# A mixture-of-experts stage regrouped from units of 64 rows on two column halves to units of 32 rows on four column quarters

## The reference

```python
logits = xt @ router_w + router_b            # 32 experts
top_v, top_i = lax.top_k(logits, 4)          # 4 experts a token: 2048 rows in all
gates = softmax(top_v)
# for every expert e and its rows xb:
gu = xb @ w_gate_up[e] + b_gate_up[e]        # 1024 -> 2048, gate and linear interleaved
act = x_glu * sigmoid(1.702 * x_glu) * (x_lin + 1)      # both clipped at 7
out = act @ w_down[e] + b_down[e]            # 1024 -> 1024
# out rows times their gates, summed back to the tokens
```

## Time and profile before

| | |
|---|---|
| median of 3 runs | 1922.38 us |
| span of the profiled execution | 1919.6 us, which leaves 2.8 us around it |
| PE (matmul) busy | 1788.8 us, 93% |
| PEld (weight load) busy | 1106.8 us, 58% |
| DVE busy | 1025.5 us, 53% |
| ACT busy | 795.8 us, 41% |
| POOL busy | 236.5 us, 12% |
| mean DMA rate over the span | 270 GB/s, 494.10 MB read |

### The profile page before, as it was taken

One profiled execution on the slowest core, in us unless ns is written; L12 is line 12 of the kernel. 1 busy time (PEld: TensorE's weight loads), 2 busy tenths in 40 slices (PEclk: granted clock), 3 DMA queues, 4 the chain that ended last, 5 costly groups with the idle time before them and its releaser, 6 DMA issues. The chain is left out here.

```text
span 1919.6 us, 41921 instructions
## 1 busy us (share of the span) xinstructions
PE 1788.8 (93%) x14459; PEld 1106.8 (58%) x14459; DVE 1025.5 (53%) x1632; ACT 795.8 (41%) x1163; POOL 236.5 (12%) x302
## 2 busy tenths in 40 slices
PE   6999888599999999999999899999999769998897
PEld 3999654455555555555554455555555336777763
DVE  5794435554554555544544345545454473874655
ACT  5335523244444444444443344444444433533411
POOL 0000000111111111111111011111111220350000
PEclk9999999699999999999999899999999879999999
DMA  8881771449878997997599998999999662221011
GB/s 328 271 263 45 197 236 43 180 158 406 356 284 318 423 379 284 363 427 324 206 406 427 426 427 338 421 427 372 405 427 426 260 211 68 77 77 46 21 40 44
DMA packets 129708, 520.06 MB, mean 271 GB/s; under 512 B 13618, under 2 KB 52291, under 8 KB 80355
## 3 DMA queue, kind: packets, MB, share of 16 engines
q1 hardware_dynamic: 116754, 483.41, 64.3%
q0 software_dynamic: 12736, 35.17, 4.9%
q10 hardware_dynamic: 146, 0.48, 0.1%
HBM read 494.10 MB, written 24.90 MB: 270 GB/s over the span
## 5 line engine op out<-in xcount | busy, mean ns | idle before, releaser
L1893 DVE COPY ring<-staging 128x2048 f32 (+1 forms) x385 | 475.2, 1234 | 506.8 <-PE banks L1754 307.8
L1754 PE MATMUL banks<-ring,rowsT 128*64 128x256 f32 x6144 | 700.9, 381 | 3.2 <-ACT rowsT L1843 3.2
L1754 PEld LDWEIGHTS banks<-ring,rowsT 128*64 128x64 f32 x6144 | 443.4, 138 | 310.5 <-issue 78.7
L1825 ACT ACTIVATE ring<-staging 128x2048 f32 (+1 forms) x193 | 369.0, 1912 | 338.6 <-PE banks L1754 274.7
L1780 PE MATMUL banks<-ring,hiddenT 128*64 128x512 f32 x1536 | 375.4, 610 | 0.5 <-PEq L1811 0.3
L1780 PEld LDWEIGHTS banks<-ring,hiddenT 128*64 128x64 f32 x1536 | 93.7, 137 | 137.3 <-issue 113.0
L1831 ACT ACTIVATE glu<-banks 128x128 f32<-128x128 f32 x192 | 53.2, 277 | 281.5 <-DVE lin L1899 281.5
L601 PE MATMUL banks<-w_in_hi,hT 128*128 128x256 f32 (+1 forms) x768 | 147.3, 291 | 1.6 <-issue 1.6
L2227 PE MATMUL banks<-h3T,w_in_hi 128*128 128x512 f32 x400 | 130.5, 408 | 1.4 <-DVE h3T L2403 1.4
L601 PEld LDWEIGHTS banks<-w_in_hi,hT 128*128 128x128 f32 x768 | 122.5, 194 | 3.6 <-issue 3.5
L1707 POOL DMA_DIRECT2D expert_rows<-y_rows x94 | 52.4, 558 | 532.5 <-ACT y_rows L1849 531.5
(11 more groups left out here) (413 smaller groups left out, 1796.6 us busy)
## 6 DMA issues: line engine op xcount, KB each, us to landing
staging<-in_w_gate_up SPq DMA_DIRECT2D x250, 1024.0 KB, 12.6
staging<-in_w_down SPq DMA_DIRECT2D x128, 1024.0 KB, 12.6
stage<-in_w_mod SPq DMA_DIRECT2D x21, 1024.0 KB, 6.1
stage<-in_w_in SPq DMA_DIRECT2D x25, 512.0 KB, 4.1
expert_rows<-y_rows POOLq DMA_DIRECT2D x94, 128.0 KB, 5.8
stage<-in_w_in SPq DMA_DIRECT2D x11, 1024.0 KB, 6.2
expert_rows<-catT SPq DMA_DIRECT2D x1, 7936.0 KB
early<-in_w_gate_up SPq DMA_DIRECT2D x6, 1024.0 KB, 11.2
```

What stands on the lines that cost most here:

```text
L1754: mm = pe.matmul(k.bank(j % 2)[c * SLOTS:(c + 1) * SLOTS, 0:UP], rowsT[:, kk, half, :], w[:, kk * WIDE + c * UP:kk * WIDE + (c + 1) * UP], ...
L1825: act.activation(ring[:, pos % RING, :], staged(e, c), ACT.Copy).then_inc(act_filled, 1)
L1893: dve.tensor_copy(ring[:, pos % RING, :], staged(e, c)).then_inc(dve_filled, 1)
```

## The change

Units have 32 rows (`SLOTS` = 32), at most 94 of them. The four column quarters of the array work at once: quarter c takes the same 32 rows and a fourth of the features. One step is a whole unit: eight up chunks of 128 input features, with matmuls of 512 columns in each quarter, then the four down chunks of the unit before, with matmuls of 256 columns. In every chunk quarter 0 is read straight from `staging` (an address computed in PE's registers), and DVE and ACT copy only the other three (1536 of 2048 floats) to the ring. `staging` has 18 slots, and a slot is free when PE is done with it in the expert's last unit. DVE fills positions 0, 1, 3, 4, 6, 8, 9, 11 and ACT 2, 5, 7, 10. The rows come as quarter rows of 1 KB, and y goes out in one DMA. POOL no longer loads a pick column: the router makes `k.lane`, a row of experts by unit. Bias is two matmuls of 512 columns (high and low part) after the sum of the unit before. The first unit reads the early slabs in place, and they are copied to `staging` during it. `gate2` is written to HBM in the router stage and read back in the second block, and some buffers share memory.

```diff
-SLOTS = 64
+SLOTS = 32
+QUARTERS = 4
-STAGED = 16
+STAGED = 18
+PART = CHUNK // QUARTERS
+GLU = PART // 2
...
-BY_DVE = (0, 2, 3, 5, 6, 8, 9, 11)
-BY_ACT = (1, 4, 7, 10)
+BY_DVE = (0, 1, 3, 4, 6, 8, 9, 11)
+BY_ACT = (2, 5, 7, 10)
...
+        def staged(i, e, c, first, size):
+            if isinstance(i, int) and i == 0 and c < EARLY:
+                return k.early_slab(c)[:, first:first + size]
+            at = (e * (CHUNKS // 2) + c // 2) % BLOCKS
...
+            return staging[:, bass.ds(at * (2 * CHUNK) + (c % 2 * CHUNK + first), size)]
...
+                def free(c, last):
+                    if c < KT:
+                        sp.wait_ge(chunk_done, last * CHUNKS + (c + 1))
                     else:
+                        sp.wait_ge(chunk_done, last * CHUNKS + (CHUNKS + c + 1))
...
+                def gather(i, out=rows, at=0):
+                    code = pool.value_load(k.table[0:1, bass.ds(i + P, 1)], min_val=0, max_val=CODES - 1)
+                    if out is rows:
+                        after(pool, rows_in, 16 * i)
+                        after(pool, rows_ps, i)
+                    pool.tensor_copy(slot[:, at:at + 1], k.slots[:, bass.ds(code, 1)]).then_inc(slot_ready, 1)
...
                 def store_rows(n):
                     pool.wait_ge(y_read, n)
-                    for part in range(2):
-                        pool.dma_start(rows_of(part, n * SLOTS - SLOTS), y[part * SLOTS:(part + 1) * SLOTS, :]
-                                       ).then_inc(y_out, 16)
-                    pool.wait_ge(y_out, 32 * n)
+                    pool.dma_start(store_of(n * SLOTS - SLOTS), y[:]).then_inc(y_out, 16)
+                    pool.wait_ge(y_out, 16 * n)
                     pool.sem_inc(y_free, 1)
...
                 with pool.Fori(1, units) as i:
-                    load_picked(i + 1)
-                    gather(i + 1)
+                    gather(i + 2)
                     store_rows(i)
...
+                def up(i, e, qs=range(KT)):
...
+                        filled(pe, i, q)
+                        row = slice(q // 2 * SLOTS, (q // 2 + 1) * SLOTS)
+                        for c in range(QUARTERS):
+                            w = ring[:, q % RING, (c - 1) * PART:c * PART] if c else staged(i, e, q, 0, PART)
+                            mm = pe.matmul(k.bank(0)[c * SLOTS:(c + 1) * SLOTS, :], rowsT[:, q % 2, row], w,
...
+                def down(n, i, e):
+                    for m in range(4):
+                        if m == 0:
+                            pe.wait_ge(hT_ready, n + 1)
+                            after(pe, y_read, n)
+                        filled(pe, i, KT + m)
+                        for b in range(2):
+                            for c in range(QUARTERS):
...
                 with pe.Fori(1, units) as i:
-                    steps(i)
+                    up(i, expert_on(pe, i))
+                    down(i - 1, i, expert_on(pe, i - 1))
+                    turn_hidden(i)
+                    turn_rows(i + 2)
+                    add_bias(i + 1)
...
                 with act.Fori(1, units) as i:
+                    e = expert_on(act, i)
+                    fill(i, e, 5)
+                    fill(i, e, 7)
+                    fill(i, expert_on(act, i - 1), 10)
+                    gate(i)
+                    rows_turned(i + 1, i * CHUNKS + KT)
+                    fill(i + 1, expert_on(act, i + 1), 2)
+                    read_y(i - 1, i * CHUNKS + CHUNKS)
+                    hidden_turned(i)
...
                 with dve.Fori(1, units) as i:
+                    e = expert_on(dve, i)
+                    fill(i, e, 3)
+                    fill(i, e, 4)
+                    pick_expert(i + 1)
+                    fill(i, e, 6)
+                    e_before = expert_on(dve, i - 1)
+                    fill(i, e_before, 8)
+                    fill(i, e_before, 9)
+                    linear(i)
+                    fill(i, e_before, 11)
+                    finish_hidden(i)
+                    e_next = expert_on(dve, i + 1)
+                    fill(i + 1, e_next, 0)
+                    fill(i + 1, e_next, 1)
```

More of the change, by code:

```diff
@@ L245, in stage_front @@
     nc, d = k.nc, k.d
+    k.gate2 = k.sb("gate2", [P, D], at=front)
     k.mod = k.sb("mod", [P, 4, D], at=front)
@@ new lines, in _ @@
+                sp.dma_start(quarter[:], d["quarters"]).then_inc(quarter_in, 16)
+                for m in range(EARLY - AHEAD):
+                    arrived(m)
+                for m in range(EARLY, NE * CHUNKS):
+                    e, c = m // CHUNKS, m % CHUNKS
+                    old = m - STAGED
+                    if old >= 0:
+                        if old % CHUNKS == 0 or old == 0:
+                            of = old // CHUNKS
+                            last = sp.value_load(k.table[0:1, ENDS + of:ENDS + of + 1], min_val=0, max_val=NBLK - 1)
+                        free(old % CHUNKS, last)
+                    sp.dma_start(staging[:, m % STAGED * CHUNK:(m % STAGED + 1) * CHUNK],
+                                 up(e, c) if c < KT else down(e, c - KT)).then_inc(raw_in[m % STAGED], 16)
+                    arrived(m - AHEAD)
@@ L1681, in _ @@
+                for m in range(NE * CHUNKS - AHEAD, NE * CHUNKS):
+                    arrived(m)
+                end = sp.value_load(k.table[0:1, TABLE - 2:TABLE - 1], min_val=NE - 1, max_val=NBLK - 1)
+                sp.wait_ge(y_read, end + 1)
+                sp.dma_start(store_of(end * SLOTS), y[:]).then_inc(last_out, 16)
+                sp.wait_ge(last_out, 16)
             @block.gpsimd
@@ L1811, in _, with add_bias @@
-                pe.sem_inc(chunk_done, 2)
-                down(end + 3, units, 3)
+                def add_bias(i):
+                    pe.wait_ge(pick_ready, i + 1)
+                    first = not (isinstance(i, int) and i == 0)
+                    if first:
+                        pe.wait_ge(lin_ready, i)
+                        pe.wait_ge(glu_ready, i)
+                    for part in range(2):
+                        mm = pe.matmul(k.bank(0), pick[:], bias[:, part, :], start=first and part == 0,
+                                       stop=not first and part == 1, skip_group_check=True)
+                    mm.then_inc(pick_used, 1)
@@ L1874, in _ @@
-                end = PAIRS * last
-                hidden_turned(end + 2, 2, last * CHUNKS + 9)
-                gate(end + 3, 3)
-                hidden_turned(end + 3, 3, units * CHUNKS)
+                act.activation(bias[:, 0, :], raw_bias, ACT.Copy).then_inc(bias_high, 1)
+                fill(0, 0, 5)
+                for m in (1, 3, 5):
+                    act.wait_ge(chunk_done, m + 1)
+                    act.activation(own_slot(m), k.early_slab(m), ACT.Copy).then_inc(settled, 1)
+                fill(0, 0, 7)
```

467 lines of the change are left out of this document (184 added, 283 removed).

## The result

The changed kernel takes 2094.44 us (median of 4 runs, 2087.43 to 2098.68) against 1922.43 beside it: a ratio of 1.088, 95% interval 1.086 to 1.091. That is 172 us more where the forecast was 35. The direction and the place were right, the size was not, and the time lies outside the range.

What follows compares the result with a forecast made beforehand. PE was taken to bound the kernel, DMA next. PE work 928, row stalls with clock 197, weight waits 45, unit 0 8 and last hidden and down 4 made a 1182 us stage; time 1957, range 1855 to 2040.

Steps and rivals of the forecast that it cites:

- PE's own work, with unit 0: PE in the expert stage: 80 units of 11.6 us, 928, plus 8 for unit 0 at half clock.
- stalls for rows: PE before row transposes: POOL's 15.8 us chain runs 4.0 past its cover while weights flow, 33 times.
- clock behind them: PE after each stall for rows: lower granted clock adds 2.0 us, bounds 0 and 3.5.
- waits for weights: PE at experts of one or two units: waits of 16 and 1.5 us, less chunks loaded ahead, some 45.
- Four column tiles: PE's up and down matmuls: four tiles stream like two, 10.64 us a unit; no-gain rival: 2575 us, chance 0.04.
- weight loads stand alone: Rival, PE matmuls: column-tile weight loads don't overlap running matmuls, 4.5 us a unit, 358 in all; time 2120, chance 0.03.
- the store lands after ... one store for two, so 5.4: POOL's store of y: landing takes 2.4 us with DMA little used, 5.6 when full; 5.4 taken.
- The other links: Rest of POOL's chain: y read 1.6, store issue 0.7, loop to slot copy 1.3, gather issue 1.0, landing 5.8 us.
- 82% of the time, every second unit: Stall count: weights flow in 977 of about 1190 us, every second unit stalls then, so 33 of 80.
- None where DMA is idle: Sign, PE before row transposes: idle of 3 to 5 us at 400 GB/s or more, none where DMA is idle.
- longer chain: Rival, POOL's chain: gather's hold or address work adds 2 us, 35 stalls of 8; time 2027, chance 0.14.
- Rows in time: Rival, POOL's chain: under 11.8 us, rows don't stall PE and DMA bounds short experts; time 1859, chance 0.29.

Runs made afterwards that it cites:

- e6_late_wait_half_weights: Changed kernel with POOL waiting for the store's landing only after the next gather, and weight transfers after the first 18 loading half their columns: 1759.54 us, ratio 0.914.
- e2_flat_store: Changed kernel with its store of y as one flat transfer of 128 rows of 1 KB to one contiguous stretch: 2002.98 us, ratio 1.041.
- e3_late_wait: Changed kernel with one wait moved: POOL waits for the landing of a store of y only after issuing the next gather: 1916.58 us, ratio 0.996.
- e9_whole_ring: e3_late_wait with no quarter read in place: ring of whole chunks, 16 staged slots, a slot free after the expert's last unit has filled: 1952.63 us, ratio 1.015.

## Why the prediction was wrong in size

The forecast's stage was 1182 us. By its own terms, with what the changed kernel shows:

| term | predicted | measured |
|---|---|---|
| PE's own work, with unit 0 | 928 + 8 | 938 (e6_late_wait_half_weights, clock 0.99) |
| stalls for rows | 33 x 4.0 = 131 | 234.5 in 41 waits, of which 35 are over 1 us |
| clock behind them | 33 x 2.0 = 66 | 1036 - 938 = 98 |
| waits for weights | 45 | 37 |
| last hidden and down, small waits | 4 | 10 |
| stage | 1182 | 1317 |

- **Four column tiles** stream as two do, an up chunk in 0.86 us (two fours of records at 0.43), and a unit without a stall lasts 11.5 us (1153.90 to 1165.42 between hidden transposes), with 11.6 predicted. That rival is out. So is *weight loads stand alone*: loads of 0.11 us (L1750) lie beside matmuls whose fours follow each other every 0.21 us, and 938 us leave no room for the rule's 358. Here the measurement decides against the line of the Trainium skill (TensorE: Matmul & The Clock Gate, "The mechanism") by which a load overlaps only where the row group differs. The same section also lets a load go ahead into a background weight buffer, which these numbers do not contradict.
- **The step that failed is "the store lands after ... one store for two, so 5.4".** It landed in 8.6 in the median of the stage and 8.9 in 1100 to 1200. The rows of before gave the landing of a plain 64-row store, and I carried it over to a transfer with another destination pattern: a row can't price a form that it doesn't have. This is the term that needed bounds from both sides, and got none above. e2_flat_store, with the form undone, measures 5.7 in the same stretch, and this one term is 91 of the 137 us by which the time missed.
- **The other links** were 1.6, 0.7, 1.3 (loop and table), 1.0 and 5.8 us by forecast, and 1.3, 0.7, 1.6, 1.8 and 6.4 in the stall shown: 1.4 us more in sum. So the chain was 20.45 for 15.8, and e2_flat_store would still have missed by 46 us.
- **How many stall.** "82% of the time, every second unit" gave 33. Of the 41 waits 35 are over 1 us and the other six 0.4 or less, so the number was about right and the size was not: 6.6 us each where 4.0 was taken. "None where DMA is idle" was nearly right. In a stretch where the DMA engines hardly ran (a share of 0.09), below, PE waits twice, 0.27 and 0.30 us, and the store lands in 4.1; in between, at 500 to 890 us, stalls of 4 us stand beside those of 8.

```profile
985.00:1017.00 32.00, 30.71 (x370) 12.79 (x363) 22.58 (x31) 19.04 (x22) 7.04 (x8) 1.00 0.09 24
```

- **The clock** cost 98 us in 35 stalls, 2.8 each where 2.0 was taken; that is 32 us more. In e3_late_wait there are no stalls of that kind, and PE's busy time is still 1006 - 938 = 68 us over what it needs.
- **Register addresses** at nothing: right within 10 us. **DMA**: not what bounds the changed kernel (a share of 0.78, 37 us of waits for fills), and in e3_late_wait the next limit, as foreseen.
- The rival *longer chain* had the right mechanism and sign, though it named other links (the gather's hold of POOL, address work) and not the landing of the store. It took 35 stalls of 8 us, 6 of waiting and 2 of clock; the 35 measured 6.6 and 2.8, so its 2027 was too low. *Rows in time* (1859) is what e3_late_wait makes of the kernel; it came to 1917, and 40 of the 58 us are the clock, on which I had put 28 where 68 were lost.
- **The start.** The forecast let the stage begin at 372.6; PE turned its first rows at 376.06, after 11.89 us of waiting for the gather, and the first up matmul began at 377.22, where the kernel before has 377.76. So the 5 us that it gave back there did not come.

## What to carry to other kernels

When work is cut into shorter units, list what each unit still waits for in a fixed time, above all an in-order queue that waits for one transfer before it issues the next: its cover shrinks with the unit and its landings don't. Move the wait for a landing to the place where the buffer is needed next, behind the next issue; that was worth 178 us here, a little more than the whole 172 that the change cost. A transfer in a new form has no price in the old trace, and a queue that "waits 500 us" has only that divided by its turns to spare.

## What the runs showed of the hardware

- A store on POOL's queue with a rearranged destination, of the same bytes and the same element size as a flat one, lands 3.2 us later under full DMA load (8.9 for 5.7) and has 96 small packets more; the shortest landings of the two kernels are 3.7 and 2.0. Written as 2 KB elements of 64 rows by two, it lands 13 us later than two plain stores, with 432 small packets more. What in the form takes the time was not tested alone.
- In e3_late_wait PE lost 68 us of clock, with 86 waits for fills of 1.3 us on average (the longest 5.9); the changed kernel lost 98 with 35 stalls of 6.6. For each us of waiting the short waits cost no less (about 0.5 with all small waits counted, for 0.4).
- POOL's issue of the same store took 1280 ns instead of 823 where DVE was busy 847 us of the stage instead of 682 and ACT 704 instead of 573 (e9_whole_ring, e3_late_wait); which of the two engines slows it was not tried.
